# Changing which weight rows share a partition in the 32-expert loop of a transformer block

## The reference, cut to what matters

```python
def clamped_swiglu(gu):
    gate = jnp.minimum(gu[..., :D_EXPERT], SWIGLU_LIMIT)
    up = jnp.clip(gu[..., D_EXPERT:], -SWIGLU_LIMIT, SWIGLU_LIMIT)
    return (up + 1.0) * (gate * jax.nn.sigmoid(gate * SWIGLU_ALPHA))

def step(acc, blk):                      # one block of an expert's tokens
    tok, g, e = blk
    xb = h_pad[tok]
    act = clamped_swiglu(xb @ w_gu[e] + b_gu[e])
    yb = act @ w_down[e] + b_down[e]
    return acc.at[tok].add(yb * g[:, None].astype(yb.dtype)), None
```

## Time and profile before

| | us |
|---|---|
| median of 3 runs | 2346.08 (2345.17 to 2347.21) |
| the profiled execution | 2347.21 |
| its span, first to last instruction | 2345.4 |
| PE busy | 2114.1 (90%) |
| DVE busy | 1062.4 (45%) |
| ACT busy | 676.6 (29%) |

### The profile page before, as it was taken

One profiled execution on the slowest core, in us unless ns is written; L12 is line 12 of the kernel. 1 busy time (PEld: TensorE's weight loads), 2 busy tenths in 40 slices (PEclk: granted clock), 3 DMA queues, 4 the chain that ended last, 5 costly groups with the idle time before them and its releaser, 6 DMA issues.

```text
span 2345.4 us, 30238 instructions
## 1 busy us (share of the span) xinstructions
PE 2114.1 (90%) x12462; PEld 1424.3 (61%) x12462; DVE 1062.4 (45%) x1546; ACT 676.6 (29%) x837; POOL 77.6 (3%) x50
## 2 busy tenths in 40 slices
PE   7988899989999999999999998697799989958998
PEld 7988797863333333333333332584599888947996
DVE  6996755452222222222222222653555565365554
ACT  4434453421111111111111111443333344333332
POOL 0241201000000000000000000000000000000000
PEclk9989999989999999999999999898799989979999
DMA  9525567578999999999999999458455545414552
GB/s 313 186 100 180 180 216 280 193 287 359 428 429 428 429 428 429 428 428 428 429 429 429 428 429 397 148 210 296 144 180 171 190 152 188 144 36 144 180 180 81
DMA packets 181642, 652.74 MB, mean 278 GB/s; under 512 B 6673, under 2 KB 70161, under 8 KB 156593
## 3 DMA queue, kind: packets, MB, share of 16 engines
q1 hardware_dynamic: 181552, 651.44, 71.2%
HBM read 650.37 MB, written 1.05 MB: 278 GB/s over the span
## 4 chain that ended last, share of the span: by engine, by line
PE 55%; DMA 31%; DVE 10%; ACT 2%; issue 2%; POOL 0%; SPq 0%; DVEq 0%; ACTq 0%; POOLq 0%
DMA ring<-w_down 29%; PE bank L710 26%; PE bank L730 12%; PE pair L969 6%; PE bank L942 3%; DVE ring_low L1732 3%; DVE arena L1782 2%; PE bank L775 1%; PE pair L775 1%; ACT w_high L1265 1%; DMA ring<-ada_w 1%; PE pair L923 1%; PE bank L742 1%; PE pair L751 0%; DVE arena L1796 0%
## 5 line engine op out<-in xcount | busy, mean ns | idle before, releaser
L1732 DVE TENSOR_TENSOR ring_low<-ring,w_high 128x2048 fp32r<-128x2048 f32 x180 | 412.4, 2295 | 372.9 <-ACT w_high L1265 371.5
L710 PE MATMUL bank<-x_high,w_high 128*128 128x256 f32 x1728 | 499.6, 289 | 40.4 <-DVE ring_low L1732 27.7
L710 PE MATMUL bank<-x_low,w_high 128*128 128x256 f32 x1728 | 495.7, 287 | 0.0
L710 PE MATMUL bank<-x_high,ring_low 128*128 128x256 f32 x1728 | 495.5, 287 | 0.0
L942 PE MATMUL bank<-ring,arena 128*64 128x512 f32 x2048 | 457.7, 595 | 18.1 <-DMA ring<-w_gu 17.2
L1265 ACT ACTIVATE w_high<-ring 128x2048 fp32r<-128x2048 f32 x180 | 339.7, 1891 | 238.3 <-PE bank L730 117.4
L710 PEld LDWEIGHTS bank<-x_high,w_high 128*128 128x128 f32 x1728 | 339.1, 196 | 46.1 <-issue 31.4
L2073 DVE TENSOR_TENSOR arena<-bank,par 128x512 f32<-128x512 f32 x64 | 43.9, 687 | 665.5 <-PE bank L952 665.5
L710 PEld LDWEIGHTS bank<-x_low,w_high 128*128 128x128 f32 x1728 | 339.2, 196 | 0.6 <-issue 0.5
L710 PEld LDWEIGHTS bank<-x_high,ring_low 128*128 128x128 f32 x1728 | 338.7, 196 | 0.0
L942 PEld LDWEIGHTS bank<-ring,arena 128*64 128x64 f32 x2048 | 141.9, 137 | 323.5 <-issue 267.1
(11 more groups left out here) (281 smaller groups left out, 1989.6 us busy)
## 6 DMA issues: line engine op xcount, KB each, us to landing
ring<-w_gu SPq DMA_DIRECT2D x128, 2048.0 KB, 24.9
ring<-w_down SPq DMA_DIRECT2D x64, 2048.0 KB, 25.4
ring<-ada_w SPq DMA_DIRECT2D x24, 2048.0 KB, 8.6
ring<-ffn_w_gate_up SPq DMA_DIRECT2D x44, 1024.0 KB, 7.7
ring<-ret_w_in SPq DMA_DIRECT2D x12, 2048.0 KB, 7.9
ring<-w_in SPq DMA_DIRECT2D x10, 2048.0 KB, 8.1
ring<-w_in SPq DMA_DIRECT2D x16, 1024.0 KB, 10.1
ring<-ffn_w_down SPq DMA_DIRECT2D x8, 2048.0 KB, 7.9
```

The lines of the kernel that those rows point to most:

```text
L710: mm = pe.matmul(acc_bank[:, ch * T:(ch + 1) * T], w[:, k, ch * P:(ch + 1) * P], xs[:, kk, :], start=kk + ch + n == 0, stop=kk == b.kc - 1 ...
L1732: V.tensor_tensor(low_part(u), raw_part(u), high_part(u).bitcast(F32), ALU.subtract).then_inc(sem("w_low"), 1)
```

## The change

The pattern of both loads becomes "(k p) n -> p k n". Partition p of a gate/up tile now takes rows p and 128 + p of the tile's 256, two pieces of 8 KiB that lie 1 MiB apart; partition p of a down tile takes rows p, 128 + p, 256 + p and 384 + p, four pieces of 4 KiB that lie 512 KiB apart. The transposes take neighbouring columns instead of every second or fourth, and the bias is regrouped on the host. Each engine has the same instructions in the same order, in the same number; in SP's list the shape of each load's source changes from 128 x 4096 to 128 x 2 x 2048 (gate/up) and 128 x 4 x 1024 (down). Sizes, waits and slots stay.

```diff
             def gu_tile(e, k):
                 src = a["w_gu"][0][e, 2 * P * k:2 * P * (k + 1), :]
-                sp.dma_start(gu_ring[k], src.rearrange("(p k) n -> p k n", p=P)).then_inc(mloaded[k], 16)
+                sp.dma_start(gu_ring[k], src.rearrange("(k p) n -> p k n", p=P)).then_inc(mloaded[k], 16)
 
             def down_tile(e, k):
                 src = a["w_down"][0][e, 4 * P * k:4 * P * (k + 1), :]
-                sp.dma_start(down_ring[k], src.rearrange("(p k) n -> p k n", p=P)).then_inc(mloaded[4 + k], 16)
+                sp.dma_start(down_ring[k], src.rearrange("(k p) n -> p k n", p=P)).then_inc(mloaded[4 + k], 16)
...
             def turn_inputs(it):
                 pe.wait_ge(sem("m_xg"), it + 1)
                 for c in range(4):
-                    pairs_of = xg_s[:, 2 * P * (c // 2):2 * P * (c // 2 + 1)].rearrange("p (m j) -> p j m", j=2)
-                    mm = pe.transpose(bank[6][:, c * P:(c + 1) * P], pairs_of[:, c % 2, :], ident)
+                    mm = pe.transpose(bank[6][:, c * P:(c + 1) * P], xg_s[:, c * P:(c + 1) * P], ident)
                 mm.then_inc(sem("m_xturn"), 1)
...
             def turn_halves(it):
                 for b in range(2):
                     pe.wait_ge(sem("m_gus"), it * 2 + (b + 1))
-                    fours = gu_s[b].rearrange("p (m j) -> p j m", j=4)
                     for c in range(4):
-                        mm = pe.transpose(bank[2 + b][:, c * P:(c + 1) * P], fours[:, c, :], ident)
+                        mm = pe.transpose(bank[2 + b][:, c * P:(c + 1) * P], gu_s[b][:, c * P:(c + 1) * P], ident)
                     mm.then_inc(sem("m_guturn"), 1)
...
-    cols["b_gu"] = np.asarray(inputs["b_gu"])[0].reshape(NEXP, 2, 2, P, 4).transpose(3, 0, 2, 4, 1).reshape(P, -1)
+    cols["b_gu"] = np.asarray(inputs["b_gu"])[0].reshape(NEXP, 2, 2, 4, P).transpose(4, 0, 2, 3, 1).reshape(P, -1)
```

## The result

The changed kernel takes 2365.16 us (median of 4 runs, 2365.11 to 2367.87) where the kernel before takes 2345.62 (4 runs): a ratio of 1.0086, with a 95% interval from 1.0068 to 1.0103. It is slower by 19.5 us; 24.4 were forecast.

A forecast was written before the change was run, and what follows sets the result against it. The full DMA queue was taken to bound the expert stage from 541 us on. Gate/up 10.1, down 14.7 and transposes -0.4 sum to +24.4 us: 2370.5 us on the median of 2346.1, range 2361 to 2379.

The forecast's parts named there:

- Rival B: Expert stage: PE is the true limit, so removing strided reads saves up to 22 us, result about 2324; chance 0.02.
- The price of a packet: Expert weight loads: each packet costs one engine 10.2 ns beside 37.6 ns per KiB, a line from 4 and 16 KiB.
- The terms 10.1 and 14.7: Added queue time in us: 124 gate/up tiles at 0.081 more each, 60 down tiles at 0.244 more each.
- The mixed row of 418 GB/s: Gate/up bound from a stretch of mostly 8 KiB packets: 5.017 us per tile, 15.1 us in all, result 2375.5.
- What is hidden: Expert 0's six tiles and the last two down tiles cost 0; without cover about 1.3 us.
- Transposes: PE's 12 contiguous transposes save up to 0.7 us per expert, mostly lengthening waits; on the path -0.4 us (0 to -0.7).
- Spare time: PE's spare time per expert grows from 2.8 to about 4.3 us, spread over six waits.
- rival E: Expert stage: longer waits make PE's clock fall, a period of 35.2 us, result about 2503; chance 0.02.
- Rival A: Expert loads: packets overlap, so a third of the price is paid, 8 us, result 2354; chance 0.05.
- Rival D: Main memory dislikes pieces 1 MiB or 512 KiB apart: 96 us more, 2442; chance 0.05, including results between it and forecast.
- Rival C: Expert stage: packet price is nil and PE has no say, so no change, 2345.7 us; chance 0.03.
- term 4: SP's issue of loads: 0.33 us for 128 packets, 0.37 for 1024, against 4.9 us per tile; costs 0.

The follow-up runs named there:

- turns_only: Kernel before with the change's contiguous transposes and regrouped bias but its own old loads; 2346.17 us against 2346.45, ratio 1.0001.
- light_after: Changed kernel with half of the gate/up bytes left unloaded from expert 1 on; 2266.55 us.
- light_before: Kernel before with half of the gate/up bytes left unloaded from expert 1 on; 2271.95 us.
- gu_32k: Kernel before with two neighbouring gate/up slots loaded by one 4 MiB DMA, 32 KiB per partition, for experts 1 to 31; 2349.14 us against 2345.69, ratio 1.0010.
- gu_32k_late: Like gu_32k, but expert 1's gate/up tiles still loaded slot by slot, pairs from expert 2 on; 2343.68 us against the kernel before's 2346.24, ratio 0.9987.
- after_again: The changed kernel measured once more against 17 runs of the kernel before; 2368.34 us against 2346.45, ratio 1.0093.
- down_near: Kernel before with a down partition's four 4 KiB pieces 8 KiB apart instead of side by side; 2359.66 us against 2345.69, ratio 1.0058.
- all_2k: Kernel before with every expert tile loaded in packets of 2 KiB, 1024 per tile; 2441.15 us against 2345.69, ratio 1.0413.
- down_only: Kernel before with only the down half of the change: 4 KiB packets, its transposes, regrouped bias; 2362.01 us against 2346.45, ratio 1.0069.
- gu_only: Kernel before with only the gate/up half of the change: 8 KiB packets and contiguous input transposes; 2353.76 us against 2346.45, ratio 1.0030.

## Why the prediction was right

1. **What bounds.** "From 541 us on tile n lands at the start plus n tile times, whatever PE does": the 184 tiles took 927.6 and 927.3 us in two profiles that began them 3.2 us apart, with a full DMA line and longer waits of PE. Rival B, PE as the limit, is out for this kernel, by turns_only. It holds for another one: light_after is 5.4 us faster than light_before, where the queue has room.
2. **The price of a packet.** Forecast 10.2 ns, from stretches of 4 and 16 KiB. Measured 9.5 and 9.4 (the halves), 9.3 (2 KiB), 8.8 (32 KiB). The 4 KiB stretch of the earlier trace rows was 3 us long, and its 408 GB/s was a little low: a down tile's 4.895 + 0.225 = 5.12 us are 409.6 GB/s. The terms 10.1 and 14.7 become 124 x 0.076 = 9.4 and 60 x 0.225 = 13.5 us, together 22.9 where the stretch from first issue to last landing grew by 22.4 and 22.7. For gate/up, the one without a clean row, the line had 0.081 us per tile and 0.076 were measured. The mixed row of 418 GB/s was too dear by more than half: its 5.017 us per tile stands against 4.971 measured.
3. **What is hidden.** The first six tiles and the last two were counted as nothing. The first six are loaded ahead of the stretch. For the last two, PE's last 32 down products begin 12.8 us after the last landing in the chain both before (1457.98 - 1445.14) and after (1478.00 - 1465.23), so they cost nothing.
4. **SP's issue.** Right as to time, wrong as to how: see the last section.
5. **Transposes.** I bounded PE's gain by the difference of weight loads, 0.7 us per expert; it is 26.59 - 26.37 = 0.22. A load mostly runs beside the product before it, so most of the 61 ns each would not be PE's time; this is argued from the rows and was not tested by itself. The -0.4 us of the sum for the transposes on the path is too small for these runs: turns_only measured -0.3 us, with an interval of some 2 us to either side.
6. **Spare time.** The waits grew to 170 us, by 53 where some 40 were forecast, and the longest is 2.2 us where 2.5 was expected. The clock stayed at 1.00 from 541 to 1445 us; rival E did not appear in the changed kernel. Its mechanism is not far off: in gu_32k the granted clock fell to 0.81 after a wait of 2.64 us, while in gu_32k_late it stayed at 1.00 after the same wait.

Of the 4.9 us between 24.4 and the first measurement's 19.5, 2 us are the packet price. The rest lies outside the stretch of the 184 tiles, as far as the profiles tell: there the first profile of the change is 4.7 us shorter than the one before (2.5 ahead of the stretch, 2.2 behind it; these two executions are 17.9 us apart, and not 19.5). I take the 2.5 us as scatter, since after_again begins its stretch as late as the kernel before, and measures 21.9. Rival A wanted a third of the price, and the packets cost 92% of it. Rival D fell by down_near. Rival C fell by the result. The Trainium skill's rule of about 3 cycles per packet ("DMA: Bandwidth & Descriptors", section "Why small descriptors are slow (HBM only)"), worth an estimated 8.7 us, agrees with these runs in that each packet has a price of its own, and gives less than half of its size: the stretch grew by 22.4 us. Where in the engine the price arises, no run here shows. That a transfer runs at line rate from 512 B up (the same page, "Specifications") is not so here: 2 KiB packets gave 387 GB/s against 428 for 16 KiB.

## What to carry to other kernels

Where the DMA queue is full and sets the pace, count packets: each cost about 9 ns (8.8 to 9.5) of one of 16 engines beside its bytes, at every size from 2 to 32 KiB, and alike for pieces 8 KiB and 512 KiB apart. Choose which rows share a partition so that a partition's share is one contiguous stretch, and let the transposes that regroup the inputs read with a stride, since PE has the time. Where PE leads and the queue has room, the choice turns round, and is worth less: 5.4 us here against 21.9.

## What was not expected of the hardware

SP is held in its issues when many packets are outstanding. One issue took 0.33 us in the kernel before, with five tiles of 128 packets in the queue. In the changed kernel an issue of down can take 2.3 us, and in all_2k SP is hardly ever free: four issues of gate/up take 21.4 us, as long as four tiles take to move. These are SP's rows of the changed kernel and of all_2k:

```profile
897.04 2.29 SPq L627 DMA_DIRECT2D ring<-w_down  x1
```

```profile
906.90 21.44 SPq L623 DMA_DIRECT2D ring<-w_gu  x4
```

A row of several issues also spans what lies between them, so the second row alone proves nothing: in the kernel before, four issues of 0.33 us make a row of 13 us, because SP waits for slots. What settles it is SP's waits from 657 to 1440 us. The kernel before has these two, and all_2k has none:

```profile
SPq L623 <- PE bank L942: 446.1, 104, 5.9
SPq L627 <- PE pair L969: 230.0, 53, 4.4
```

It is not the packets of the issue itself that count. In down_only a gate/up load is still 128 packets, and its issue can take 3.9 us behind the 512-packet loads of down; in gu_only, with 256 packets per gate/up load, issues take 0.38 us at most. The kernel before held an issue in the same way, the third of three for the second block's weights; the prediction's term 4 took the 0.37 us of an issue into an empty queue instead.

The first row below is of down_only, the second of the kernel before.

```profile
876.46 3.94 SPq L623 DMA_DIRECT2D ring<-w_gu  x1
```

```profile
1452.27 7.12 SPq L601 DMA_DIRECT2D ring<-att_w_qkv  x1
```

A load of all_2k lands 19.7 us after its issue began (median) where one of the kernel before needs 24.9, though each tile takes longer: fewer tiles fit in the queue ahead of it. It cost nothing here, because the queue stayed full (387 GB/s throughout). A kernel whose SP has other transfers to issue might pay for it; no run here tests that.
